# Splitting all 34 weight tiles once and loading every one of them in tile 1

## Chip, core and metric

One Trainium2 chip, one core. The metric is the device time of one execution in microseconds (us), the median of several executions. TensorE is called PE, VectorE DVE, ScalarE ACT, GpSimd POOL; SP is the queue that issues nearly all DMAs.

## What is computed

A block of a streaming encoder on 2048 positions and 1024 channels, in float32. Cut to what matters:

```python
h = rmsnorm(x, w_norm_pre)
proj = h @ w_in                       # 1024 x 3328: 26 weight tiles
q_a, k_a, v_a, z_a, q_r, f_r, i_r, z_r = jnp.split(proj, SPLIT_POINTS, axis=-1)
o_a = sliding_window_sink_attention(rope(q_a), rope(k_a), v_a, sinks) * silu(z_a)
o_r = rmsnorm(hgrn2_chunkwise(q_r, f_r, i_r, lb), hgrn_norm) * silu(z_r)
y = concat([o_a, o_r]) @ w_out        # 1024 x 1024: 8 weight tiles
x = x + rmsnorm(y, w_norm_post)
```

## The kernel before

The sequence is cut into 4 tiles of 512 positions (`t` from 0 to 3). Each tile passes over the weights, which are cut into weight tiles of 128 partitions x 1024 elements (0.5 MB): 26 of `w_in` (steps 0 to 25) and 8 of `w_out` (steps 26 to 33). In tiles 2 and 3 the output projection runs over 14 prepared tiles instead of 8 (`FAST`). A matmul of full float32 precision is made of three in the rounded type fp32r: every operand is split into a high half (rounded) and a low half (the rest), and the products high x high, low x high and high x low are summed in PSUM. One step is 24 matmuls of 512 columns (L596; L605 for `w_out`), with small matmuls of attention and recurrence put between them by `between`.

**Weight tiles are numbered through:** i = 34 t + w in tiles 0 and 1. A tile that is split passes through these hands:

- `load_raw(i)` (L445, issued by SP): the float32 tile goes from DRAM to one of 4 raw slots. It first waits until tile i - 4 has been split.
- `split_hi(i)` (L919, ACT, instruction L924): the high half is rounded into slot `SPLIT_SLOT[i]` of `w_hi`. It waits for three things: that PE has finished with the tile that had the slot before (`wait_slot`, L384), that this tile's halves have landed in DRAM if they are saved (`wait_saved`, L379), and that the raw tile has landed.
- `split_lo(i)` (L1257, DVE, instruction L1263): raw minus high goes to the same slot of `w_lo`.
- `save_split(i)` (L453, SP, issues L458): both halves are written to the DRAM tensors `kept_hi` and `kept_lo`, two DMAs of 0.5 MB. It waits for the split.

From number `FRESH` on, tiles aren't split. `load_split` (L461, SP, issues L469) loads both halves back from `kept`, two DMAs of 0.5 MB, after the same two waits, `wait_slot` and `wait_saved`. PE waits for one or the other in `wait_split` (L396).

There are 4 slots for halves. In tile 0 from tile 28 on only three of them are used: tiles 28, 29, 30 are in slots 0, 1, 2, so are 31, 32, 33, and the first three of tile 1 (34, 35, 36) take slots 0, 1, 2 again; 37 takes slot 3, which tile 27 had. The early waits of PE in tile 1 are thus for slots that became free three steps before.

Before, `LATE` is 6: saves begin with tile 6, and tile 1 splits its first six tiles (34 to 39) a second time and then saves them as rows 0 to 5 of `kept`. In tile 1's step 6 (i = 40 = `FRESH`) the loads begin.

**The order on SP** is that of the program and nothing passes anything else. For every i it holds `load_raw(i)`, then `save_split(i - 4)`, then, from `FRESH` on, `load_split`. Between them stand the tables of rope (at step 4 of tile 0, L499 and L500), the next tile's x (from step 10) and the residual rows (L512), whose first half is issued at step 31 of tile 0 and waits for DVE's L1253 in step 28.

ACT and DVE also run in program order. ACT does the splits of step s in `splits(t, s)` (L148): tile 34 at step 32 of tile 0, 35 at step 33, 36 and 37 after the squares of y at the end of tile 0 (L1225), 38 and 39 in steps 1 and 2 of tile 1. Five stores of the output of tile 0 (L1232, 2 MB in all) are issued on ACT's own DMA queue after those of 36 and 37.

The core of the program of SP:

```python
def load_raw(i):
    if i >= RAW_SLOTS:
        sp.wait_ge(lo_split.sem, lo_split.after(0, 0) + i - RAW_SLOTS)
...
def wait_saved(engine, i):
    slot = SPLIT_SLOT[i]
    engine.wait_ge(w_saved[slot], 32 * uses(slot, LATE, min(i, FRESH)))
```

Of the kernel before, what the change touches and what calls it, by code (L numbers as in the profile page):

```python
# [55 lines left out]
RAW_SLOTS = 4  # L56
# [22 lines left out]
def index(t, w):  # L79
    return t * WT + w if t < FAST else FAST * WT + (t - FAST) * FAST_WT + w  # L80
# [7 lines left out]
def tiles_of(t):  # L88
    return WT if t < FAST else FAST_WT
# [52 lines left out]
def split_at(s):  # L142


    return [w for w in (s + 2, s + 3) if w - s == (2 if w % WT in (0, 1, 2, 31, 32, 33) else 3)]


def splits(t, s):  # L148

    return [t * WT + w for w in split_at(s) if 3 < t * WT + w < FRESH]  # L150


LATE = 6
FRESH = WT + LATE

DVE_LOW = range(4, FRESH)
# [33 lines left out]
def hybrid_block(nc, x, x_rows, weights, cos, sin, vectors, w_post, squares, out, kept):  # L190
# [3 lines left out]
    with ctx:  # L194
# [180 lines left out]
        def uses(slot, start, end):  # L375

            return SPLIT_SLOT[start:end].count(slot)
# [6 lines that stand above are left out]
# [49 lines left out]
        def _(sp):  # L433
            def load_x(tile, k):


                if k == 0:
                    sp.wait_ge(h_lo_done.sem, h_lo_done.after(tile - 1, -1))
                    sp.wait_ge(x_squared.sem, x_squared.after(tile - 1, -1))
                    sp.wait_ge(finished.sem, finished.after(tile - 2, -1))  # L440
                    sp.wait_ge(finished_pool.sem, finished_pool.after(tile - 2, -1))
                sp.dma_start(x_in[:, k:k + 2, :],
                             x[bass.ts(tile, P), k * N:(k + 2) * N].rearrange("p (k n) -> p k n", n=N)).then_inc(x_quarter[k // 2], 16)
# [5 lines that stand above are left out]
                w, slot = i % WT, i % RAW_SLOTS  # L449
                sp.dma_start(w_raw[:, slot, :, :],  # L450
                             weights[w * P:(w + 1) * P, :].rearrange("p (k m) -> p k m", k=KT)).then_inc(w_loaded[slot], 16)

            def save_split(i):  # L453

                w, slot = i % WT, SPLIT_SLOT[i]
                sp.wait_ge(lo_split.sem, lo_split.after(0, 0) + i)
                for part, rows in ((w_hi, kept[0]), (w_lo, kept[1])):
                    sp.dma_start(rows[w * P:(w + 1) * P, :].rearrange("p (k m) -> p k m", k=KT),  # L458
                                 part[:, slot, :, :].bitcast(FP32)).then_inc(w_saved[slot], 16)

            def load_split(tile, w):  # L461

                slot, row = SPLIT_SLOT[index(tile, w)], rows_of(tile, w)
                wait_slot(sp, index(tile, w))
                wait_saved(sp, index(tile, w))
                if w == P7A and tile == FAST:
                    sp.wait_ge(t_saved, 16 * 2 * T_TILES)
                for part, rows in ((w_hi, kept[0]), (w_lo, kept[1])):
                    sp.dma_start(part[:, slot, :, :].bitcast(FP32),  # L469
                                 rows[row * P:(row + 1) * P, :].rearrange("p (k m) -> p k m", k=KT)).then_inc(w_ready[slot], 16)  # L470

            def load_sums(j):

                if j == 0:
                    sp.wait_ge(lo_split.sem, lo_split.after(0, 0) + FRESH - 1)
                else:
                    sp.wait_ge(t_saved, 16 * T_TILES)
                for r, w in enumerate((B11, B21, B12, B22)):
                    sp.dma_start(w_raw[:, r, :, :], weights[(w + j) * P:(w + j + 1) * P, :].rearrange("p (k m) -> p k m", k=KT)).then_inc(t_raw, 16)

            def save_sums(j, first):

                sp.wait_ge(t_high, 4 * j + first + 2)
                sp.wait_ge(t_low, 4 * j + first + 2)
                for r, w in ((0, T1), (2, T3)) if first == 0 else ((3, T2), (1, T4)):
                    rows = slice((w + j) * P, (w + j + 1) * P)
                    sp.dma_start(kept[0][rows, :].rearrange("p (k m) -> p k m", k=2), t_hi[j][r].bitcast(FP32)).then_inc(t_saved, 16)
                    sp.dma_start(kept[1][rows, :].rearrange("p (k m) -> p k m", k=KT), w_raw[:, r, :, :]).then_inc(t_saved, 16)
# [8 lines left out]
            def load_tables(t):  # L497
                sp.wait_ge(roped.sem, roped.after(t - 1, -1))
                sp.dma_start(cos_t[:, :], cos[bass.ts(t, P), :]).then_inc(tables_loaded, 16)  # L499
                sp.dma_start(sin_t[:, :], sin[bass.ts(t, P), :]).then_inc(tables_loaded, 16)  # L500
# [32 lines left out]
            for t in range(TILES):  # L533
                for w in range(tiles_of(t)):
                    i = index(t, w)
                    if FIRST_SPLIT <= i < FRESH:
                        load_raw(i)
                    if LATE + RAW_SLOTS <= i <= FRESH:
                        save_split(i - RAW_SLOTS)
                    if i == FRESH + 1:  # L540
                        for late in range(FRESH + 1 - RAW_SLOTS, FRESH):
                            save_split(late)
                    if i >= FRESH:
                        load_split(t, w)
                    if t == 0 and w == RAW_SLOTS:
                        load_tables(0)
                    if w - H0 in range(0, KT, 2) and t + 1 < TILES:
                        load_x(t + 1, w - H0)
                    if w == OUT0 and t + 1 < TILES:
                        load_tables(t + 1)  # L550
                    if (t, w) in SUMS_IN:
                        load_sums(SUMS_IN.index((t, w)))
                    for j in range(2):
                        for first in (0, 2):
                            if (t, w, first) in SUMS_OUT[j]:
                                save_sums(j, first)
                    if w == 1 and t > FAST:
                        load_residual(t - 1, 0)
                        load_residual(t - 1, 1)
                    if w == RAW_SLOTS - 1 and t > FAST:  # L560
                        store_y(t - 1, STORES)
                    if w == RES_AT[t][0]:
                        load_residual(t, 0)
                    if w == RES_AT[t][1]:
                        load_residual(t, 1)
# [6 lines left out]
        def _(pe):  # L572
# [219 lines left out]
            def unit_waits(t, n, w, k, i):  # L792

                if w not in [v for v, _, _ in UNITS[:n]]:
                    wait_split(pe, t, w)
# [442 lines left out]
        def _(dve):  # L1238
# [18 lines left out]
            def split_lo(i):  # L1257
                dve.wait_ge(hi_split.sem, hi_split.after(0, 0) + i)
                if i in (DVE_LOW.start, DVE_LOW.stop):

                    dve.wait_ge(lo_split.sem, lo_split.after(0, 0) + i - 1)
                s = SPLIT_SLOT[i]
                dve.tensor_tensor(w_lo[:, s, :, :], w_raw[:, i % RAW_SLOTS, :, :], w_hi[:, s, :, :], ALU.subtract).then_inc(lo_split.sem, 1)  # L1263
# [265 lines left out]
            for t in range(TILES):  # L1529
                links[0] = 0  # L1530
                for s in range(WT):
                    q, odd = divmod(s - SCORES0, 2)
                    h_of, kind = divmod(s - 1 - H0, 4) if H0 < s <= OUT0 else (0, None)
# [116 lines left out]
                            sum_head(t, h)  # L1650
                    if t == FAST and 0 <= s - SUMS_AT < 4:
                        sum_weights(1, s - SUMS_AT)
                    for i in splits(t, s) if (t, s) != (1, 0) and (t or kind not in (0, 1)) else ():
                        if i in DVE_LOW:
                            split_lo(i)

# [10 lines left out]
                for b in range(4):  # L1667
                    if b == 3 and t + 1 < TILES:
                        dve.wait_ge(x_high, t + 1)
                        dve.tensor_tensor(mix_lo[:, 0, :], x_acc[:, :], mix_hi[:, 0, :], ALU.subtract).then_inc(x_low, 1)  # L1670
                    if b == 3 and t == 0:
                        for i in splits(1, 0):
                            split_lo(i)
                    copy_y(t, 1, b)
                    if b == 0:
                        dve.wait_ge(res_loaded, t * 32 + 32)
                    dve.wait_ge(y_rstd.sem, y_rstd.after(t, b))
                    dve.wait_ge(y_read.sem, y_read.after(t, 4 + b))
                    for half in range(b in Y_POOL, 2):
                        finish_y(t, b, half)  # L1680
# [129 lines left out]
```

## Time and profile before

| | |
|---|---|
| median of 3 executions | 864.86 us (864.5 to 866.69) |
| profiled execution, its own time | 864.57 us |
| span of its instructions | 862.7 us |
| outside the span | 1.87 us |
| instructions | 12445 |
| moved by DMA | 211.20 MB |

The span runs from the first to the last instruction of the profiled execution; 1.87 us of its own time lie outside it. The profiled execution lies 0.29 us under the median. The timeline view gives starts in us from the span's start. Landing times are given by the DMA view as us from issue to landing.

### The profile page before, as it was taken

The page shows a single profiled execution, that of the slowest core. Times are in us where ns is not written, and L with a number is a line of the kernel's source. Part 1 is how long each engine was busy: PE and PEld are TensorE (multiplying, and loading weights), DVE is VectorE, ACT ScalarE, POOL GpSimd, SP SyncE. Part 2 cuts the span into 40 slices and gives each one's busy share as a digit, 9 for nine tenths or more (in the row PEclk, how much of TensorE's full clock was granted, in tenths as well). Part 3 has the DMA queues.
Part 4 walks back from the last instruction along what each step waited for, and adds up shares of the span by engine and source line. Part 5 has one row for each costly group of instructions (what it writes and reads, how often), then busy time and mean ns, then how long its engine had stood idle before and what let it go on. Part 6 is the DMA issues. An engine that isn't in the chain of part 4 may idle for free.

```text
span 862.7 us, 12445 instructions
## 1 busy us (share of the span) xinstructions
PE 851.9 (99%) x4428; PEld 700.6 (81%) x4428; DVE 631.9 (73%) x1125; ACT 519.0 (60%) x1033; POOL 114.6 (13%) x84
## 2 busy tenths in 40 slices
PE   8999999999999999999999999999999999999997
PEld 6787788888888778888888878888888887888885
DVE  6878878674656799767747789887775368888846
ACT  7766445763466458567446655865853755576544
POOL 0000013430200000332020000144300000004220
PEclk9999999999999999999999999999999999999999
DMA  8686755748986647464898785445699674444586
GB/s 322 212 325 221 244 205 170 285 147 314 418 342 248 213 145 265 152 210 133 321 382 348 276 330 172 146 151 216 241 374 396 228 273 147 147 147 158 189 326 254
DMA packets 59981, 211.20 MB, mean 245 GB/s; under 512 B 6672, under 2 KB 6928, under 8 KB 59920
## 3 DMA queue, kind: packets, MB, share of 16 engines
q1 hardware_dynamic: 57904, 205.56, 65.3%
q10 hardware_dynamic: 2016, 4.85, 1.4%
q8 instruction: 35, 0.57, 0.3%
q14 instruction: 26, 0.21, 0.1%
HBM read 157.95 MB, written 52.43 MB: 244 GB/s over the span
## 4 chain that ended last, share of the span: by engine, by line
PE 84%; DVE 9%; ACT 4%; issue 3%; DVEq 0%
PE bank L596 55%; PE bank L605 5%; PE turn_b L852 3%; PE score_b L852 3%; PE bank L852 3%; PE score_b L605 3%; PE turn_b L605 3%; PE turn_b L653 2%; DVE kv_tok L1386 2%; PE score_b L629 2%; PE turn_b L706 2%; PE bank L697 1%; PE bank L687 1%; PE turn_b L709 1%; ACT probs_t L951 1%
## 5 line engine op out<-in xcount | busy, mean ns | idle before, releaser
L596 PE MATMUL bank<-h_hi,w_lo 128*128 128x512 f32 x832 | 326.9, 393 | 0.0
L596 PE MATMUL bank<-h_lo,w_hi 128*128 128x512 f32 x832 | 326.3, 392 | 0.0
L596 PE MATMUL bank<-h_hi,w_hi 128*128 128x512 f32 x832 | 324.4, 391 | 0.5 <-issue 0.5
L596 PEld LDWEIGHTS bank<-h_lo,w_hi 128*128 128x128 f32 x832 | 156.4, 188 | 34.7 <-issue 3.3
L596 PEld LDWEIGHTS bank<-h_hi,w_hi 128*128 128x128 f32 x832 | 156.4, 188 | 33.1 <-issue 1.0
L596 PEld LDWEIGHTS bank<-h_hi,w_lo 128*128 128x128 f32 x832 | 156.3, 188 | 32.8
L1716 POOL TENSOR_TENSOR mix_lo<-v_r,mix_hi 128x512 fp32r<-128x512 f32 x16 | 21.2, 1322 | 539.0 <-ACT v_r L1142 539.0
L1263 DVE TENSOR_TENSOR w_lo<-w_raw,w_hi 128x1024 fp32r<-128x1024 f32 x36 | 44.8, 1248 | 34.6 <-ACT w_hi L924 34.1
L1386 DVE STREAM_TRANSPOSE kv_tok<-k_mid 32x128 f32<-32x128 f32 x192 | 58.1, 303 | 2.8
L924 ACT ACTIVATE w_hi<-w_raw 128x1024 fp32r<-128x1024 f32 x38 | 39.8, 1051 | 24.9 <-issue 10.2
L1700 POOL TENSOR_TENSOR x_acc<-x_acc,x_sq 128x512 f32<-128x512 f32 x21 | 32.7, 1557 | 70.0 <-ACT x_sq L974 70.0
L928 ACT ACTIVATE g_a<-g_b 128x512 f32<-128x512 f32 x30 | 18.9, 630 | 38.2 <-DVE g_b L1340 38.2
L939 ACT ACTIVATE g_a<-g_a 128x512 f32<-128x512 f32 x32 | 20.2, 632 | 34.6 <-DVE g_a L1344 34.6
L1068 ACT ACTIVATE f_b<-bank 32x512 f32<-32x512 f32 x48 | 28.3, 589 | 15.6 <-PE bank L596 9.7
L960 ACT ACTIVATE kv_tok<-f_d 32x128 f32<-32x128 f32 x96 | 29.5, 307 | 10.0 <-DVE f_d L1580 8.9
L1344 DVE SCALAR_TENSOR_TENSOR g_a<-g_b,g_a 128x512 f32<-128x512 f32 x30 | 21.7, 723 | 18.3 <-ACT g_a L930 18.3
L960 ACT ACTIVATE probs<-f_d 32x128 f32<-32x128 f32 x96 | 29.5, 307 | 1.2
L1637 DVE TENSOR_TENSOR_SCAN f_c<-reset,f_b 128x512 f32<-128x512 f32 x16 | 19.6, 1225 | 11.3 <-ACT f_b L1125 11.3
L1479 DVE SCALAR_TENSOR_TENSOR q_gate<-q_gate,y_stats,x_in 128x512 f32<-128x512 f32 x28 | 23.1, 873 | 4.4 <-DMA x_in<-in_x_rows 3.5
L605 PE MATMUL bank<-w_hi,mix_lo 128*128 128x512 f32 x64 | 25.3, 395 | 0.0
L605 PE MATMUL bank<-w_hi,mix_hi 128*128 128x512 f32 x64 | 24.9, 390 | 0.0
L605 PE MATMUL bank<-w_lo,mix_hi 128*128 128x512 f32 x64 | 24.9, 389 | 0.0
(280 smaller groups left out, 1549.2 us busy)
## 6 DMA issues: line engine op xcount, KB each, us to landing
w_hi<-kept_hi SPq DMA_DIRECT2D x108, 512.0 KB, 3.8
w_lo<-kept_lo SPq DMA_DIRECT2D x108, 512.0 KB, 4.9
w_raw<-in_weights SPq DMA_DIRECT2D x46, 512.0 KB, 6.2
kept_hi<-w_hi SPq DMA_DIRECT2D x34, 512.0 KB, 6.3
kept_lo<-w_lo SPq DMA_DIRECT2D x34, 512.0 KB, 7.4
x_in<-in_x_rows SPq DMA_DIRECT2D x8, 1024.0 KB, 8.1
x_in<-in_x SPq DMA_DIRECT2D x15, 512.0 KB, 6.6
kept_lo<-w_raw SPq DMA_DIRECT2D x8, 512.0 KB, 7.0
```

The source lines that it names most:

```text
L596: mm = pe.matmul(acc(w)[:, :], stationary[:, s, k, :], moving[:, k, :], start=(m == 0), stop=(m == 3 * KT - 1), skip_group_check=True)
L605: mm = pe.matmul(y_bank[half][b][:, :], mix[:, k, b * P:(b + 1) * P], weight[:, SPLIT_SLOT[index(t, w)], (k % 2) * 4:(k % 2) * 4 + 4, :].r ...
L852: mm = pe.matmul(into, mix, weight, start=w in (P1A, P7A, P2A, P4A) and k == 0 and part == 0, stop=k == KT // 2 - 1 and part == 2, skip_gr ...
L924: act.activation(w_hi[:, SPLIT_SLOT[i], :, :], w_raw[:, i % RAW_SLOTS, :, :], ACT.Copy).then_inc(hi_split.sem, 1)
L960: copy = act.activation(square(v_tok(t, h), j, i), square(f_d[:, :], i, j), ACT.Copy)
L1068: copy = act.activation(dst[32 * b:32 * b + 32, :], acc(s - 1)[32 * (b ^ 1):32 * (b ^ 1) + 32, :], ACT.Copy)
L1263: dve.tensor_tensor(w_lo[:, s, :, :], w_raw[:, i % RAW_SLOTS, :, :], w_hi[:, s, :, :], ALU.subtract).then_inc(lo_split.sem, 1)
L1344: dve.scalar_tensor_tensor(g_a[:, :], g_b[:, :], 0.0, gate_log(t, i), ALU.min, ALU.subtract).then_inc(gate_arg.sem, 1)
L1386: last = dve.transpose(square(kv_tok[:, 0, :], j, i), square(k_mid[:, :], i, j))
L1479: dve.scalar_tensor_tensor(y, y, y_scale[:, b:b + 1], x_in[:, 2 * b + half, :], ALU.mult, ALU.add).then_inc(finished.sem, 1)
L1700: pool.tensor_tensor(x_acc[:, :], x_acc[:, :], x_sq[:, :], ALU.add).then_inc(x_added.sem, 1)
L1716: pool.tensor_tensor(o_sq_lo, o_sq[:, :], o_sq_hi, ALU.subtract).then_inc(o_low.sem, 1)
```

## The change

`LATE` becomes 0 and so `FRESH` 34: the saves begin with tile 0, and every tile from 34 on is loaded. All 34 saves are of tile 0's splits; those of tiles 0 to 5 are issued in its steps 4 to 9. The last four saves are placed anew: 30 and 31 at i = 34 ahead of the load of 34, 32 at i = 35 ahead of the load of 35, 33 at i = 36 ahead of the load of 36. The split code for tile 1 goes.

```diff
-LATE = 6
+LATE = 0
 FRESH = WT + LATE
...
                     if LATE + RAW_SLOTS <= i <= FRESH:
                         save_split(i - RAW_SLOTS)
-                    if i == FRESH + 1:
-                        for late in range(FRESH + 1 - RAW_SLOTS, FRESH):
-                            save_split(late)
+                    if FRESH <= i < FRESH + 3:
+                        save_split(i - 3)
                     if i >= FRESH:
                         load_split(t, w)
...
-                    for i in splits(t, s) if (t, s) != (1, 0) and (t or kind not in (0, 1)) else ():
+                    for i in splits(t, s) if t or kind not in (0, 1) else ():
                         if i in DVE_LOW:
                             split_lo(i)
...
-                    if b == 3 and t == 0:
-                        for i in splits(1, 0):
-                            split_lo(i)
```

## Rows read from the trace of the kernel before

**Rows 1.** The page, busy time by engine and the chain that ended last.

```profile
PE 851.9 (99%) x4428; PEld 700.6 (81%) x4428; DVE 631.9 (73%) x1125; ACT 519.0 (60%) x1033; POOL 114.6 (13%) x84
...
PE 84%; DVE 9%; ACT 4%; issue 3%; DVEq 0%
```

**Rows 2.** PE's waits: us in total, times, longest us.

```profile
PE bank L861 <- DVE ones_r L1265: 3.5, 1, 3.5
```

**Rows 3.** Timeline of PE, first matmuls of steps 0, 1, 2 of tile 1 (start us, us).

```profile
226.28 0.39 PE L596 MATMUL bank<-h_hi,w_hi 128*128 128x512 f32 x1
...
231.72 0.39 PE L596 MATMUL bank<-h_hi,w_hi 128*128 128x512 f32 x1
...
237.62 0.39 PE L596 MATMUL bank<-h_hi,w_hi 128*128 128x512 f32 x1
```

**Rows 4.** The page, costliest groups: the two instructions of a split.

```profile
L1263 DVE TENSOR_TENSOR w_lo<-w_raw,w_hi 128x1024 fp32r<-128x1024 f32 x36 | 44.8, 1248 | 34.6 <-ACT w_hi L924 34.1
...
L924 ACT ACTIVATE w_hi<-w_raw 128x1024 fp32r<-128x1024 f32 x38 | 39.8, 1051 | 24.9 <-issue 10.2
```

**Rows 5.** Timeline of SP, end of tile 0: low half of the save of 31.

```profile
210.31 0.43 SPq L458 DMA_DIRECT2D kept_lo<-w_lo  x1
```

**Rows 6.** DMAs issued from 209.4 to 210.5 us: count, KB, us to landing.

```profile
kept_lo<-w_lo SPq DMA_DIRECT2D x1, 512.0 KB, 11.0
```

**Rows 7.** Timeline of ACT: the split of tile 34, [idle before <- releaser].

```profile
221.37 1.06 ACT L924 ACTIVATE w_hi<-w_raw 128x1024 fp32r<-128x1024 f32 x1 [2.69 <-DMA kept_lo<-w_lo]
```

**Rows 8.** Windows view, 198 to 240 us: busy of each engine, clock, DMA share, GB/s.

```profile
198.00:240.00 42.00, 42.00 (x187) 34.79 (x186) 22.41 (x28) 16.63 (x36) 5.74 (x4) 1.00 1.01 402
```

**Rows 9.** DMAs issued from 264.9 to 265.5 us: one pair of loads alone.

```profile
w_hi<-kept_hi SPq DMA_DIRECT2D x1, 512.0 KB, 3.7
w_lo<-kept_lo SPq DMA_DIRECT2D x1, 512.0 KB, 5.2
```

**Rows 10.** DMAs issued from 61.4 to 62.4 us: a raw load with a save behind it.

```profile
w_raw<-in_weights SPq DMA_DIRECT2D x1, 512.0 KB, 4.2
...
kept_lo<-w_lo SPq DMA_DIRECT2D x1, 512.0 KB, 5.9
```

**Rows 11.** A save issued between 228.6 and 232.5 us; the page's median; the first store of y.

```profile
kept_lo<-w_lo SPq DMA_DIRECT2D x1, 512.0 KB, 8.6
...
kept_lo<-w_lo SPq DMA_DIRECT2D x34, 512.0 KB, 7.4
...
231.12 0.35 ACTq L1232 DMA_DIRECT2D out<-q_gate  x1
```

**Rows 12.** Windows view, 12 to 40 us, columns as in rows 8.

```profile
12.00:40.00 28.00, 27.93 (x122) 22.48 (x121) 23.61 (x36) 24.46 (x39) 0.00 (x0) 1.00 0.72 255
```

**Rows 13.** DMAs issued from 12.1 to 13.1 us: raw tile 4 and a table.

```profile
w_raw<-in_weights SPq DMA_DIRECT2D x1, 512.0 KB, 4.9
```

**Rows 14.** Timelines of SP, ACT, DVE and PE, start of tile 0.

```profile
12.58 0.43 SPq L499 DMA_DIRECT2D cos_t<-in_cos  x1
...
21.11 1.05 ACT L924 ACTIVATE w_hi<-w_raw 128x1024 fp32r<-128x1024 f32 x1
...
33.82 1.06 ACT L924 ACTIVATE w_hi<-w_raw 128x1024 fp32r<-128x1024 f32 x1
...
26.47 0.69 DVE L1322 TENSOR_TENSOR cos_t<-cos_t,x_scale 128x512 f32<-128x512 f32 x1 [0.48 <-ACT x_scale L966]
...
27.80 0.69 DVE L1326 TENSOR_TENSOR f_a<-bank,cos_t 128x512 f32<-128x512 f32 x1
...
31.19 0.39 PE L596 MATMUL bank<-h_hi,w_hi 128*128 128x512 f32 x1
```

**Rows 15.** Timeline of PE at its start and its end; the last window's clock.

```profile
7.71 0.77 PE L596 MATMUL bank<-h_hi,w_hi 128*128 128x512 f32 x1
...
856.22 0.39 PE L852 MATMUL turn_b<-w_lo,s_hi 128*128 128x512 f32 x1
...
857.00:862.70 5.70, 0.00 (x0) 0.92 0.75 289
```

## The prediction

> **What bounds the kernel now.** I read the page first: PE is busy for 99% of the span, no other engine for more than 73%, and the chain that ended last is PE's for 84% [rows 1]. The view of PE's waits then shows where it stands still: the largest entry by far is one of 3.5 us, before its first instruction [rows 2]. The timeline confirms it at the place that the change touches: step 0 of tile 1 starts at 226.28 us and step 1 at 231.72, which is 24 matmuls at 0.227 us each, the pitch at which they follow each other where nothing is in their way [rows 3]. So PE computes almost without a pause. The change takes no matmul away. Anything removed from ACT, DVE or the DMA queues is worth nothing by itself; anything that makes PE wait is added in full.
>
> **What is removed.** Six splits: 6 x 1.05 = 6.3 us on ACT and 6 x 1.25 = 7.5 us on DVE [rows 4]. PE covers both, so I count 0; their cover would be gone only where PE waits, and there neither is late. Six raw loads (3 MB) go too. What gets earlier is tile 0's y: ACT no longer splits tile 34 at 221.37 us [rows 7] and 35 after it, before the second half's squares, nor 36 and 37 before the stores of the output. PE doesn't wait for those today, so this is 0 as well, but the 2 MB of stores will come some 3 us earlier than today and meet the new loads.
>
> **What is moved to the start.** Six saves (6 MB) now stand in SP's steps 4 to 9. From 198 to 240 us the DMA engines are full at 402 GB/s [rows 8]; half a megabyte takes 1.3 us at that rate, and where three such transfers follow each other the third lands 2.55 us after the first, 1.27 each [rows 10]. I take 1.25. Raw tile 4, issued 0.37 us ahead of the first table at 12.58 [rows 14], lands 4.9 us later at 17.1 [rows 13]. The save of tile 0 follows it: 17.1 + 2.5 = 19.6 us. Three may now wait for it. The tables, behind it: 19.6 + 1.25 = 20.9, and DVE reads them at 26.47. ACT's split of tile 4, which needs tile 0's slot saved, runs at 21.11. Then raw 5, save 1, raw 6, save 2, raw 7, save 3 are 9 transfers, 11.25 us: save 3 lands at 32.1, or 33.6 with the 0.6 MB that ACT's own queue loads then (masks and norm weights, L1035 and L1037), and ACT's split of tile 7 runs at 33.82 [rows 14]. Everything is in time, if closely. In the 28 us from 12 to 40 the engines are 72% busy [rows 12], so 7.8 us of the 15 us that are added find room there and the rest runs on into a stretch where each split still has four steps. I cost it at 0. The bounds: no gain; as a loss the rival on tile 0's start below.
>
> **What is new: a chain of saves and loads at the start of tile 1.** Today tiles 34 to 39 come through raw slots, whose loads need no halves slot. After the change tile 34's load must wait until tile 31's save, from the same slot, has landed. And SP issues in order: save 32 stands behind load 34, load 35 waits for save 32, save 33 stands behind load 35, and load 36 waits for save 33. Three transfers that used to lie side by side come one after the other, each with its full latency.
>
> The first link: save 31's low half is issued at 210.31 us today [rows 5] and lands 11.0 us later, at 221.3 [rows 6]; ACT's split of 34, released by a save of the low half, starts at 221.37 and confirms it [rows 7]. It queues behind raw tiles 34 and 35, which go: 221.3 - 2 x 1.25 = 218.8 us. What comes before it isn't changed: the residual rows, which hold up SP at step 31, and the saves up to 30.
>
> A pair of loads alone: the high half lands 3.7 us after its issue, the low half, issued about 0.4 later, after 5.2; 5.6 us for the pair [rows 9]. A load pair with a save pair behind it isn't in the trace with idle engines before it. The nearest is a raw load with a save, 1.5 MB: the low half, issued 0.85 us after the raw load, lands 5.9 us on [rows 10], 6.75 in all. That is 3 x 1.25 us of transfer and 3.0 us fixed. For 2 MB: 5.0 + 3.1 = 8.1 us, the 3.1 taken from the load pair (5.6 - 2.5), which is how every such link begins. Bounds for the link: 7 us (a fixed part of 2) and 9 us (some store among it).
>
> - Load 34: issued 218.8, lands 224.4. PE wants it at 226.28 [rows 3]: in time by 1.9 us.
> - Save 32 lands at 218.8 + 8.1 = 226.9. Load 35 lands at 226.9 + 5.6 = 232.5. PE wants it at 231.72: **0.8 us of waiting**.
> - Save 33: 226.9 + 8.1 = 235.0 without the output stores. Those are issued from 231.12 us on today; the save issued just ahead of them took 8.6 us against a median of 7.4, one store more [rows 11]. I take one store: 236.3. Load 36: 236.3 + 5.6 = 241.9. All that is then issued since 226.9 (load 35, save 33, stores, load 36) is 12.5 us of transfer, and 226.9 + 12.5 + 3.1 = 242.5 is when it would land if every store went first. Between both: 242.3. PE wants it at 237.62: **4.7 us in total**, of which 0.8 are already had.
>
> Tile 37 is loaded right behind 36, two transfers later, 244.8, and is wanted at 242.3 + 5.4 + a bit: in time. Tiles 38 and on have their slots free and no save to wait for. Bounds of the sum: without any store in the way 240.6, 3.0 us; with all 5 us of stores ahead of save 33, 245.7, 8.1 us. I keep 4.7, nearest to the rows that show how a save and a store mix.
>
> **Sum:** 864.57 (the profiled execution) + 0 + 4.7 = 869.3 us. It lies 0.29 us under the median, so 869.5 is what I put against 864.86, +0.5%.
>
> **Rival 1: the links are short and PE doesn't wait.** This ends on the other side. From 218.8 to 237.62 there are 18.8 us for two links and a pair of loads, which I make 21.8 and, with stores, 23.5. If the fixed part is about 1 us shorter per link than in rows 9 and 10, and stores keep out of the way, what is left is under 1 us: 865 us. For it: with nothing else in flight the engines answer faster. Against it: the pair of rows 9 had them to itself and shows 3.1 us of fixed part. 13%, a tenth of it or so below 864.9 by more than the noise. The Trainium skill, DMA: Bandwidth & Descriptors, "Latency and other measured facts", puts the fixed cost at about 2 us and says that it shrinks with the load on the memory; by its figure (an estimate) each link loses 1 us and the stall would be about 1.7 us, 866.5 us.
>
> **Rival 2: the clock falls during the stall.** PE has not stood still once before. At 7.71 us a matmul still takes 0.77 us, twice the 0.39 of later ones, so 1.2 GHz held from its first instruction at 3.5 to about 8.3 us (7.71 and one slow matmul), 4.8 us [rows 2, 15]. If the stall of about 4 us brought 1.2 GHz back, about 4.8 us would run at half speed: 2.4 us more, 872 us. Against it: after the last matmul at 856.22 the window from 857 on still shows a mean clock of 0.92 [rows 15], that is 0.9 us at half level at its end, so 5 us of standing still passed at 2.4 GHz. 10%. The Trainium skill, TensorE: Matmul & The Clock Gate, Part 1, says that an idle array goes back to half its clock; by that rule the clock could fall in a stall of this length.
>
> **Rival 3: the early saves hold up tile 0.** ACT's split of tile 4 waits for save 0. PE's step 4 needs the bank that DVE's L1326 reads at 27.80 + 0.7 and starts at 31.19: 2.7 us of room, 3.1 with DVE's idle 0.48 [rows 14]. If save 0 lands later than 24.2 us, that room is spent; a landing at 26.9 costs 2.7 us, 872 us with the rest. 8%.
>
> **The change doesn't do what it says:** the saves' number and rows stay 34 whatever the code says; I see in the diff that they do. 2%, same time.
>
> **The numbers.** The forecast (waiting of 3.0 to 8.1 us, 868 to 873) has 67%. A measurement of this kernel can tell 0.3%, 2.6 us, from nothing: up to 862.3 is faster, from 867.5 slower. Slower takes the forecast, rivals 2 and 3 and a little of rival 1: 0.85; same 0.13; faster 0.02. The range has to leave out no more than 2 in 10: from 866.0, inside rival 1, to 873.0, the far end of the stores' bound.
>
> **What would show it.** In the changed kernel's profile: PE's waits gain two entries at L596, released by DMA `w_lo<-kept_lo`, of about 0.8 and 4 us, for tiles 35 and 36, and step 2 of tile 1 starts at about 242. SP's waits show L458's landings (kept_lo) before the loads, about 8 us apart. The clock stays at 1.00. Up to 226 us every PE step starts as today, within 0.5 us. DMA moves 214 MB (211.2 + 6 - 3), and 6 splits are gone on either engine: L924 x32, L1263 x30. It is wrong if PE waits for nothing there (links short), if tile 0's steps 4 to 8 start later than today (rival 3), or if the waiting lies in a step that I call in time.

## The result and the profile after

The changed kernel takes 874.36 us (median of 6, 872.93 to 876.56) against 865.30 before (6 executions beside them); the ratio is 1.0105, 95% interval 1.009 to 1.012. It is slower by 9.1 us where 4.6 us were forecast, and lies outside the range of 866 to 873.

The profiled execution took 874.30 us with a span of 872.5 us, 9.8 more than before. The page shows the work that was forecast and a slightly smaller busy share of PE:

```profile
PE 856.0 (98%) x4428; PEld 702.7 (81%) x4428; DVE 625.9 (72%) x1119; ACT 513.6 (59%) x1027; POOL 114.6 (13%) x84
...
DMA packets 60845, 214.34 MB, mean 246 GB/s; under 512 B 6768, under 2 KB 7024, under 8 KB 60784
...
PE 71%; DVE 12%; ACT 6%; DMA 5%; issue 4%; SPq 2%; POOL 0%; DVEq 0%; ACTq 0%
...
L1262 DVE TENSOR_TENSOR w_lo<-w_raw,w_hi 128x1024 fp32r<-128x1024 f32 x30 | 37.7, 1256 | 26.9 <-ACT w_hi L923 26.4
L923 ACT ACTIVATE w_hi<-w_raw 128x1024 fp32r<-128x1024 f32 x32 | 33.6, 1051 | 15.5 <-issue 11.2
```

DMA now has a share of 5% in the chain that ended last, where it had none [rows 1], and six splits are gone on either engine [rows 4]. The view of PE's waits names what took the time (us in total, times, longest us; its entry of 3.5 us before the first instruction is as before), and that of SP's waits what stands behind it:

```profile
PE bank L595 <- DMA w_lo<-kept_lo: 5.0, 1, 5.0
PE turn_b L583 <- DMA w_lo<-kept_lo: 0.5, 1, 0.5
```

```profile
SPq L382 <- DMA kept_lo<-w_lo: 25.4, 3, 9.4
```

PE has two new waits, both for a load's low half, and SP has three for a save's landing, 25.4 us in total. They are the chain of the prediction. PE's timeline has them at the steps that the prediction named:

```profile
232.27 0.39 PE L595 MATMUL bank<-h_lo,w_hi 128*128 128x512 f32 x1
237.71 0.80 PE L595 MATMUL bank<-h_hi,w_hi 128*128 128x512 f32 x1 [5.05 <-DMA w_lo<-kept_lo]
238.30 0.63 PE L595 MATMUL bank<-h_hi,w_lo 128*128 128x512 f32 x1
...
243.42 0.57 PE L595 MATMUL bank<-h_hi,w_lo 128*128 128x512 f32 x1
...
246.79 0.50 PE L583 MATMUL turn_b<-mix_hi,ones_r 128*128 128x512 f32 x1 [0.51 <-DMA w_lo<-kept_lo]
...
247.36 0.40 PE L595 MATMUL bank<-h_hi,w_hi 128*128 128x512 f32 x1
```

Step 1 of tile 1 starts at 237.71 us instead of 231.72, step 2 at 247.36 instead of 237.62 [rows 3]. From there to the end the distance to the kernel before stays within 0.1 us of 9.8. So the ledger is: 0.8 us at the start of tile 0, 5.2 at tile 35 (step 1), 3.8 more up to step 2. The matmuls between show durations of about 0.6 us until 243.4 instead of 0.39, which is the second surprise. The windows view of that stretch (busy of PE, PEld, DVE, ACT, POOL, then granted clock, DMA share, GB/s):

```profile
232.50:237.70 5.20, 0.16 (x1) 0.00 (x0) 1.31 (x2) 2.35 (x4) 0.00 (x0) 0.93 1.02 412
237.70:242.00 4.30, 4.29 (x10) 3.43 (x11) 0.00 (x0) 0.00 (x0) 0.00 (x0) 0.50 0.70 281
242.00:244.00 2.00, 2.00 (x6) 1.54 (x6) 0.00 (x0) 0.00 (x0) 0.00 (x0) 0.55 0.51 168
244.00:247.30 3.30, 2.79 (x12) 1.99 (x12) 0.00 (x0) 0.00 (x0) 0.00 (x0) 1.00 0.97 366
```

The granted clock fell from 2.4 to 1.2 GHz in PE's wait: 0.93 as the mean of the first 5.2 us puts the fall at 237.0 us, 4.3 us after PE's last matmul had ended at 232.7. Step 1 took 8.2 us from its first matmul to its last instead of 5.2. And while PE waits, the DMA engines are full (412 GB/s). The timelines of SP and ACT's queue say with what:

```profile
220.17 0.32 SPq L469 DMA_DIRECT2D w_hi<-kept_hi  x1
...
221.48 0.43 SPq L458 DMA_DIRECT2D kept_lo<-w_lo  x1
229.06 0.32 SPq L469 DMA_DIRECT2D w_hi<-kept_hi  x1
...
232.00 0.76 SPq L458 DMA_DIRECT2D kept_lo<-w_lo  x1
241.81 0.32 SPq L469 DMA_DIRECT2D w_hi<-kept_hi  x1
```

```profile
228.37 0.35 ACTq L1231 DMA_DIRECT2D out<-q_gate  x1
```

The loads of 34, 35 and 36 are issued at 220.17, 229.06 and 241.81, each when the save before it has landed. The first store of tile 0's output is issued at 228.37, 2.8 us earlier than before [rows 11] and ahead of load 35. The DMA view for what was issued from 229.0 to 229.5, for save 33, and for load 36 (count, KB, us to landing):

```profile
w_lo<-kept_lo SPq DMA_DIRECT2D x1, 512.0 KB, 8.2
out<-q_gate ACTq DMA_DIRECT2D x1, 512.0 KB, 7.0
...
kept_lo<-w_lo SPq DMA_DIRECT2D x1, 512.0 KB, 9.8
...
w_hi<-kept_hi SPq DMA_DIRECT2D x1, 512.0 KB, 3.7
w_lo<-kept_lo SPq DMA_DIRECT2D x1, 512.0 KB, 4.6
```

Load 35's low half, issued at 229.42, lands after 8.2 us at 237.6, save 33's at 232.00 + 9.8 = 241.8, load 36's at 242.18 + 4.6 = 246.8.

### The profile page after: what moved, and what is told of

Same layout as the page of the kernel before. It is cut to its first block, busy times and chain, and to the rows that moved or that the text cites. A ratio compares the mean times of both kernels' runs of the same rounds, so it can differ in the third digit from the quotient of the medians.

```text
span 872.5 us, 12439 instructions
## 1 busy us (share of the span) xinstructions
PE 856.0 (98%) x4428; PEld 702.7 (81%) x4428; DVE 625.9 (72%) x1119; ACT 513.6 (59%) x1027; POOL 114.6 (13%) x84
## 4 chain that ended last, share of the span: by engine, by line
PE 71%; DVE 12%; ACT 6%; DMA 5%; issue 4%; SPq 2%; POOL 0%; DVEq 0%; ACTq 0%
PE bank L595 49%; DMA kept_lo<-w_lo 3%; PE turn_b L851 3%; PE score_b L851 3%; PE bank L604 2%; PE bank L851 2%; DVE kv_tok L1385 2%; PE turn_b L652 2%; PE score_b L628 2%; PE turn_b L705 1%; PE turn_b L604 1%; PE score_b L604 1%; PE turn_b L708 1%; PE bank L696 1%; PE bank L686 1%
## 5 line engine op out<-in xcount | busy, mean ns | idle before, releaser
L1262 DVE TENSOR_TENSOR w_lo<-w_raw,w_hi 128x1024 fp32r<-128x1024 f32 x30 | 37.7, 1256 | 26.9 <-ACT w_hi L923 26.4
L923 ACT ACTIVATE w_hi<-w_raw 128x1024 fp32r<-128x1024 f32 x32 | 33.6, 1051 | 15.5 <-issue 11.2
L1252 DVE SCALAR_TENSOR_TENSOR h_lo<-x_in,vec,h_hi 128x512 fp32r<-128x512 f32 x32 | 23.3, 774 | 3.4 <-ACT h_hi L977 3.4
L1339 DVE TENSOR_TENSOR g_b<-bank,x_scale 128x512 f32<-128x512 f32 x32 | 21.8, 682 | 4.7 <-PE bank L595 4.1
```

The source lines that it names most:

```text
L923: act.activation(w_hi[:, SPLIT_SLOT[i], :, :], w_raw[:, i % RAW_SLOTS, :, :], ACT.Copy).then_inc(hi_split.sem, 1)
L1252: dve.scalar_tensor_tensor(h_lo[:, k, :], x_in[:, k, :], w_pre[:, k:k + 1], h_hi[:, k, :], ALU.mult, ALU.subtract).then_inc(h_lo_done.sem, 1)
L1339: dve.tensor_tensor(g_b[:, :], acc(w)[:, :], x_scale[:, :], ALU.mult).then_inc(tile_read.sem, 1)
```

## The experiments

All but `early_saves_alone` start from the changed kernel. "Before" is run beside each group on the same chip and had medians of 864.93 to 865.20 us.

### Is it the order? Both saves ahead of the loads

```diff
-                    if FRESH <= i < FRESH + 3:
-                        save_split(i - 3)
+                    for late in {FRESH: (31, 32), FRESH + 1: (33,)}.get(i, ()):
+                        save_split(late)
```

> The changed kernel with saves 31 and 32 ahead of load 34 and save 33 ahead of load 35, so that no load stands between two saves. Theory (the chain of save, load, save, load, save, load on SP makes the loss): save 31 still lands at about 220, but save 32 lands at about 223 and save 33 at about 228; loads 35 and 36 are issued then and land before PE wants them or within 1 us of it. Time 865 to 867 us, PE's waits for w_lo<-kept_lo at most 1 us. Rival (the bytes at the boundary are what is too much, in whatever order): load 36 still lands near 246 and the time stays at 872 to 875 us.

864.90 us (864.62 to 866.45), ratio to before 1.000 (0.9991 to 1.0009). The whole loss is gone, with the same bytes. The timeline of SP in this kernel:

```profile
214.01 0.69 SPq L458 DMA_DIRECT2D kept_lo<-w_lo  x1
219.71 0.32 SPq L469 DMA_DIRECT2D w_hi<-kept_hi  x1
...
221.02 0.43 SPq L458 DMA_DIRECT2D kept_lo<-w_lo  x1
222.19 0.32 SPq L469 DMA_DIRECT2D w_hi<-kept_hi  x1
...
228.23 0.32 SPq L469 DMA_DIRECT2D w_hi<-kept_hi  x1
```

Save 32 is issued at 214.0 instead of 221.5, so load 35 goes at 222.2 and load 36 at 228.2, 13.6 us earlier than in the changed kernel. Step 2 of tile 1 starts at 238.45, 0.8 us after the kernel before [rows 3], as every step since step 4 of tile 0. Load 36's low half took 8.3 us among the same stores, and nothing waited for it. The theory holds, the rival falls.

### How large is each link? One save ahead

```diff
+                    for late in {FRESH: (31, 32), FRESH + 2: (33,)}.get(i, ()):
+                        save_split(late)
```

> The changed kernel with only save 32 moved ahead of load 34; save 33 stays between loads 35 and 36. Theory: one link of the chain is gone. Save 32 lands near 222, load 35 near 229 (wanted at 232.5), save 33 near 231 to 233, load 36 near 237 to 239 (wanted at 238.4): loss 0 to 1 us, 865 to 866.5 us. Rival (both saves must be ahead): load 36 lands at 241 or later, 868 us or more.

868.25 us (866.06 to 869.82), ratio 1.0031 (1.0018 to 1.0045). That is above the 865 to 866.5 us that I expected, and as slow as the rival's 868, though load 36 landed before the rival's 241. One link taken out brings back most of the loss, but not all. Save 33 landed at 232.0 as forecast, but load 36 behind it met the stores and took 8.5 us, landing at 240.45; PE waited 1.9 us for it:

```profile
PE turn_b L583 <- DMA w_lo<-kept_lo: 1.9, 1, 1.9
```

Step 2 of tile 1 starts 3.4 us after the kernel before, 1.2 of it from the start of tile 0. Another 0.6 us is lost late in tile 2, 0.4 of it in a wait for a weight load. Why, isn't known.

The other one alone puts save 33 behind save 32 and ahead of load 35:

```diff
+                    for late in {FRESH: (31,), FRESH + 1: (32, 33)}.get(i, ()):
+                        save_split(late)
```

> The changed kernel with save 33 moved ahead of load 35, behind save 32, which stays behind load 34. Theory: load 35 still waits for save 32, landed near 229, and lands at 235 to 237, wanted at 232.5; load 36 follows when save 33 has landed, near 231.5, so right behind load 35, and lands at 238 to 241, wanted some 5.5 us after load 35's landing. PE waits 3 to 5 us, most of it for tile 35: 868.5 to 870.5 us. Rival (only the last link counts): 865 to 866.5 us.

872.89 us (872.05 to 874.26), 3.4 us above the middle of what I expected. The landings are near the theory's (load 35 at 237.25, load 36 at 241.5), the time is not. PE waited 5.6 us for tile 35 and then nothing for 36; the windows view from the end of its standstill on (PE busy, clock, DMA share, GB/s):

```profile
237.50:241.00 3.50, 3.50 (x9) 0.50 1.04 418
241.00:246.00 5.00, 5.00 (x20) 0.80 0.79 323
```

The clock was at half until 243.0 us. Tile 36's halves were there 4.5 us before step 2 began at 245.98, so nothing hid the slow matmuls here.

### What do the output stores add?

```diff
+                    if t == 0:
+                        act.wait_ge(w_ready[SPLIT_SLOT[WT + 2]], 32)
                     for b, cols, pieces, pool_pieces in PLAIN_STORES if t < FAST else ():
```

> The changed kernel in which ACT holds tile 0's five output stores back until tile 36's halves have landed, so that none of their 2 MB meets loads 35 and 36 or save 33. Theory (chain plus stores): a load lands 5.7 us after its issue and a save 8 to 8.8 us after the load ahead of it, so load 35 lands near 234.8, save 33 near 237.5, load 36 near 242.6 and step 2 of tile 1 starts about 5 us late instead of 9.7: 869.5 to 871 us. Rival (links are long without the stores too): load 36 lands at 245 or later, 873 us or more.

869.44 us (868.69 to 871.43), 4.9 us less than the changed kernel and at the lower end of what I expected. The DMA view of the new load 35, save 33 and load 36, issued at 228.12 to 228.48, 228.96 to 230.76 and 236.32 to 236.68:

```profile
w_lo<-kept_lo SPq DMA_DIRECT2D x1, 512.0 KB, 5.3
...
kept_lo<-w_lo SPq DMA_DIRECT2D x1, 512.0 KB, 5.5
...
w_lo<-kept_lo SPq DMA_DIRECT2D x1, 512.0 KB, 4.5
```

Load 35 landed at 233.8 (5.7 us for the pair), save 33 at 236.3 (8.2 us after the save before it) and load 36 at 241.2: the theory's links, and the 240.6 us that the prediction had worked out without stores. PE waited only 1.8 us for tile 35, and the clock still fell.

Making the stores small instead of late was less clean (most of tile 0's output is left out):

```diff
+                        if t == 0:
+                            act.dma_start(out[bass.ds(b * P, P), cols[0] * N:cols[0] * N + 128],
+                                          q_gate[:, 2 * b + cols[0], 0:128]).then_inc(stored[b // 2], 16)
+                            continue
```

> The changed kernel in which the five stores of tile 0's output on ACT's queue write 64 KB each in place of 256 or 512 KB (most of tile 0's output is left out), so 1.7 MB less at the boundary. Theory (the stores lengthen two links of the chain): load 35 lands some 5.7 us after its issue instead of 8.6, save 33 lands near 237.5 instead of 241.8 and load 36 near 243 instead of 246.8; the time falls by 3.5 to 4.5 us, to 870 to 871 us. Rival (the fixed part of each link makes the loss, not the stores): less than 1 us gained, 873.5 to 875 us.

871.98 us (869.02 to 873.21), 2.4 less than the changed kernel where 3.5 to 4.5 were expected. Load 36 landed at 243.3 as the theory has it, 3.5 us earlier, but load 35 still took 7.1 us as a pair, so the small stores of 512 bytes per partition weren't free; and the profiled execution lost another 1.0 us late in tile 2, 0.7 of it in a wait for a weight load, which I leave unexplained. The direction is the theory's, the size short of it.

### Do the early saves cost anything?

The kernel before, with its first six saves early; tiles 34 to 39 are split again and not saved:

```diff
-                    if LATE + RAW_SLOTS <= i <= FRESH:
+                    if RAW_SLOTS <= i < WT + RAW_SLOTS:
                         save_split(i - RAW_SLOTS)
-                    if i == FRESH + 1:
-                        for late in range(FRESH + 1 - RAW_SLOTS, FRESH):
-                            save_split(late)
...
-            engine.wait_ge(w_saved[slot], 32 * uses(slot, LATE, min(i, FRESH)))
+            engine.wait_ge(w_saved[slot], 32 * uses(slot, 0, min(i, WT)))
```

> The kernel before, with its first six saves moved to steps 4 to 9 of tile 0 (its 34 saves are those of tiles 0 to 33); tile 1 still splits its first six tiles a second time and doesn't save them. Theory: the early saves cost nothing or up to 0.8 us at the start of tile 0 and nothing later, since each split waits for a save that has landed: 865 to 866.3 us. Rival (they hold up tile 0 or load its queues for long): tile 1 starts 2 us or more late, 867.5 us or more.

865.77 us (864.71 to 866.35), ratio 1.0003 (0.9995 to 1.0012): no difference that can be measured. Its profiled execution starts tile 1 1.3 us later than that of before, but that distance is there from step 1 of tile 0 on, ahead of anything that the early saves can delay, and shrinks by 0.3 up to step 4. Most of it is a clock that rose later at the start of the program, as PE's timeline shows, first of this kernel and then of the kernel before:

```profile
10.92 0.63 PE L593 MATMUL bank<-h_hi,w_lo 128*128 128x512 f32 x1
...
11.37 0.40 PE L596 MATMUL bank<-h_hi,w_lo 128*128 128x512 f32 x1
```

From 8.6 to 11.6 us PE did 8 matmuls here and 15 in the kernel before. The start of tile 0 varies by as much between the profiled executions of all these kernels (step 1 from 0.5 earlier to 1.5 later than before). Of the changed kernel's 0.8 us, 0.4 is there at step 1. The rest appears between 22 and 26 us, and in that stretch the other kernels with early saves, this one included, move by -0.3 to +0.3 us. So neither part is shown to be a cost of the early saves.

### Does the fallen clock cost anything?

```diff
+                    if (t, w) == (1, 1):
+                        pe.wait_ge(y_read.sem, y_read.after(1, 3 - 8))
+                        for _ in range(20):
+                            pe.matmul(acc(1)[:, :], ones_r[:, :], h_hi[:, 0, :], start=True, stop=True)
                     wait_split(pe, t, w)
```

> The changed kernel with 20 matmuls of 512 columns whose result is overwritten (4.5 us at full clock) ahead of PE's wait for tile 35's halves, so that PE doesn't stand still there for 5 us and its clock stays at 1.00. Theory (the landing of tile 36's halves at about 246.8 sets the loss, and the 3 us that PE lost at half clock lay beside that wait): the time stays within 0.5 us, 873.8 to 874.9 us, and PE waits longer for tile 36 than before, by some 3 us. Rival (the clock's fall adds to the loss): 3 us less, 871 to 871.5 us.

874.61 us (872.76 to 875.01): unchanged, as the theory has it, but the profile shows that it is no clean proof. The clock stayed full through step 1 and fell in step 2 instead, after PE's 2.7 us of waiting for tile 36, as PE's timeline shows:

```profile
245.11 0.50 PE L583 MATMUL turn_b<-mix_hi,ones_r 128*128 128x512 f32 x1 [2.73 <-DMA w_lo<-kept_lo]
...
245.91 0.42 PE L595 MATMUL bank<-h_hi,w_lo 128*128 128x512 f32 x1
246.14 0.61 PE L595 MATMUL bank<-h_lo,w_hi 128*128 128x512 f32 x1
```

Step 2 took 1.65 us longer for it, and load 36 had landed 1.7 us earlier than in the changed kernel. The two cancel. (1.1 of the 1.7 us were already there when save 31 landed, long before the fill began.) So both waits were filled, the second with 12 matmuls more:

```diff
-                    if (t, w) == (1, 1):
-                        pe.wait_ge(y_read.sem, y_read.after(1, 3 - 8))
-                        for _ in range(20):
-                            pe.matmul(acc(1)[:, :], ones_r[:, :], h_hi[:, 0, :], start=True, stop=True)
+                    if (t, w) in ((1, 1), (1, 2)):
+                        pe.wait_ge(y_read.sem, y_read.after(1, (3, 1)[w - 1] - 8))
+                        for _ in range((20, 12)[w - 1]):
+                            pe.matmul(acc(w)[:, :], ones_r[:, :], h_hi[:, 0, :], start=True, stop=True)
```

> As fill_wait, and 12 more matmuls of 512 columns (2.7 us) ahead of PE's wait for tile 36, so that its clock stays full in both waits. Theory: step 2 starts when tile 36's halves have landed, 245 to 247 us, and no matmul runs at half clock afterwards, which in fill_wait cost 1.65 us: 872.5 to 874 us, between that and the changed kernel itself because the landing sets it. Rival (the clock's fall is 3 us of the loss): 871 us or less.

872.92 us (872.09 to 874.81), clock 1.00 throughout the boundary in the profile. Within the theory's 872.5 to 874, outside the rival's 871 or less. The fill itself, at its end at 244.7, outlasts the landing at 244.2 by half a microsecond. By the medians the changed kernel takes 1.4 us less with a full clock, or 1.9 without that excess, but the intervals of the two ratios overlap (1.0081 to 1.0115 and 1.009 to 1.012), and in this profile load 36 landed 2.6 us earlier (244.2 against 246.8), 1.6 of it already at save 31's landing. So no part of the difference is shown to be the clock's; its share is at most some 2 us, not 3.

The clean case is `only_33_ahead`, where nothing waits behind the slow step. The same 20 matmuls there, added to that kernel by the same lines as in `fill_wait`:

```diff
+                    if (t, w) == (1, 1):
+                        pe.wait_ge(y_read.sem, y_read.after(1, 3 - 8))
+                        for _ in range(20):
+                            pe.matmul(acc(1)[:, :], ones_r[:, :], h_hi[:, 0, :], start=True, stop=True)
```

> only_33_ahead with 20 matmuls of 512 columns (4.5 us) ahead of PE's wait for tile 35, whose result is overwritten, so that the clock stays full. There tile 36's halves land long before PE is done with tile 35 at half clock, so no second wait hides the fall. Theory (a fall costs about 2.9 us where nothing waits behind it): tile 35 lands at about 237 as before, its step then takes 5.4 instead of 8.3 us, and the time falls by 2.4 to 3.0 us, from 872.9 to about 870 us. Rival (the landings alone set the time, as in fill_wait): within 0.7 us of 872.9.

869.92 us (869.30 to 871.36) against 872.89: 3.0 us. In the profiles the stretch from the start of step 1 to that of step 2 takes 5.9 us (236.75 to 242.65) instead of 8.7 (237.28 to 245.98), which is 2.8 us for the clock alone. The same windows of this kernel as of `only_33_ahead` above:

```profile
237.50:241.00 3.50, 3.50 (x17) 1.00 1.03 415
241.00:246.00 5.00, 5.00 (x23) 1.00 1.04 422
```

17 matmuls in 3.5 us instead of 9. The Trainium skill, TensorE: Matmul & The Clock Gate, Part 1, says that an idle array goes back to half its clock; the traces agree: 0.50 after PE stood still for 5.6 us, 1.00 where the wait was filled.

### A second cure: the fourth slot

```diff
-SPLIT_SLOT = [s for r in (4, 4, 4, 4, 4, 4, 4, 3, 3) for s in range(r)]
+SPLIT_SLOT = [i % 4 for i in range(34)]
...
-SPLIT_SLOT += [w % 4 for w in range(WT)] + [(WT + w) % 4 for w in range(FAST_WT)] * (TILES - FAST)
+SPLIT_SLOT += [(WT + w) % 4 for w in range(WT)] + [(2 * WT + w) % 4 for w in range(FAST_WT)] * (TILES - FAST)
```

> The changed kernel, its order on SP untouched, with the tiles of halves going round all four slots without a break (34 takes the slot of 30 instead of 31, 35 that of 31, 36 that of 32). Theory (a load that waits for the save issued just before it makes the chain): now each load waits for a save issued one place earlier, which has landed or is about to. Load 34 is issued near 217, load 35 near 220, load 36 near 226 and lands near 232, before it is wanted: no loss at the boundary, 865 to 866.3 us, and PE's waits show no w_lo<-kept_lo over 0.5 us. Rival (the order, save 32 and 33 behind loads, is bad by itself): 868 us or more.

866.37 us (864.55 to 866.88), ratio 1.0003 (0.9994 to 1.0012). SP's order is that of the changed kernel and the loss is gone all the same, since no load waits for the save issued just ahead of it. Load 36 goes at 224.8:

```profile
216.28 0.32 SPq L469 DMA_DIRECT2D w_hi<-kept_hi  x1
...
218.77 0.32 SPq L469 DMA_DIRECT2D w_hi<-kept_hi  x1
...
224.80 0.32 SPq L469 DMA_DIRECT2D w_hi<-kept_hi  x1
```

PE's waits name no `kept_lo` in it. Neither this nor `saves_ahead` is faster than the kernel before: PE's work is the same and it sets the time.

## Why the prediction was wrong

**Right:** PE sets the time, and what ACT and DVE lose (6 splits each) is worth nothing. The early saves cost nothing that can be measured. One sign of being wrong did appear, since tile 0's steps start 0.8 us late instead of within 0.5, but `early_saves_alone` shows no loss, and rival 3 falls. The loss is the chain save 31, load 34, save 32, load 35, save 33, load 36; tile 34 is in time, tiles 35 and 36 are late, nothing after them is, and moving two saves ahead of two loads removes all of it. Rival 1 falls too: the links aren't shorter than the 8.1 us taken from the rows, but 8.9 (save 31 to save 32) and 12.8 us (save 32 to save 33).

**Wrong, the term for the stores.** The step that failed is "I take one store". By the prediction's own steps:

| | predicted | measured | without stores (`late_y_stores`) |
|---|---|---|---|
| save 31 lands | 218.8 | 220.05 | 219.1 |
| save 32 lands | 226.9 | 229.0 | 228.1 |
| load 35 lands | 232.5 | 237.6 | 233.8 |
| save 33 lands | 236.3 | 241.8 | 236.3 |
| load 36 lands | 242.3 | 246.8 | 241.2 |

The link from save 32's landing to save 33's was put at 9.4 us and measured 12.8; with the stores held back it was 8.2. The difference of 4.6 us is nearly the 5 us that 2 MB take. I had seen that the stores come some 3 us earlier, and then priced them by the save of [rows 11]. But that save was issued ahead of every store, the first of which came at 231.12, and two more came before it landed at 237.2. The kernel before:

```profile
228.67 0.83 SPq L458 DMA_DIRECT2D kept_lo<-w_lo  x1
...
232.32 0.35 ACTq L1232 DMA_DIRECT2D out<-q_gate  x1
234.02 0.34 ACTq L1232 DMA_DIRECT2D out<-q_gate  x1
```

So the row wasn't one store met by one save, and it doesn't have the case of the changed kernel, where the stores begin ahead of load 35 (228.37 against 229.06) and of save 33 (231.18). There they land from 232.9 to 242.1 us, four of the five before save 33 at 241.8, and load 36, which isn't issued until then, can't share the time with them. My check by total bytes (242.5) had load 36 already queued while the stores ran, which the chain itself forbids. The bound that I set aside, all 5 us of stores ahead of save 33, was nearly the case: 8.1 us against 9.2 measured at load 36's landing (246.8 - 237.62), of which 0.8 is tile 0's later start.

The stores are the largest part of the miss, but not all. Load 36 landed 4.5 us after 242.3: save 31 landed 1.3 late (0.8 of it tile 0's start), the first link took 0.8 more than 8.1 without any store in it (8.9 to 9.0 us in `late_y_stores` too), the second 3.4 more than 9.4, and load 36 1.0 less than the 6.0 left for it.

**Wrong, the clock.** Rival 2 had 10% and happened. The evidence against it was the end of the program, where 5 us of standing still passed at 2.4 GHz [rows 15]; 4.3 us were enough at the boundary, and 1.8 us in `late_y_stores`. That end was one sample, and an unusual one. In the changed kernel the last matmul ends at 866.40, and the clock has fallen two microseconds later:

```profile
866.50:868.40 1.90, 0.00 (x0) 0.00 (x0) 1.90 (x4) 1.13 (x4) 0.00 (x0) 1.00 0.98 381
868.50:872.50 4.00, 0.00 (x0) 0.00 (x0) 1.52 (x3) 0.00 (x0) 0.00 (x0) 0.50 0.67 262
```

Over the ends of all twelve profiles it fell 2.0 to 5.2 us after the last matmul, and the kernel before has the longest. At the boundary the fall cost at most some 2 us, less than its price of 2.4, because PE would have waited for tile 36 in any case: at full clock step 1 would have ended near 243.1 us, 3.7 before the landing. `fill_both` gives the 2 us as a bound; where nothing hides the fall, it costs 2.8 to 3.0.

## What to carry over

Where a load reuses a buffer whose old content must first be saved, let it wait only for a save that was issued at least one load earlier, by moving the save up (`saves_ahead`) or with one more buffer (`four_slots`). A load that waits for the save just ahead of it pays the full latency of both in every round, here 8 to 13 us against a step of 5.4. When an engine is relieved, ask what its transfers will now collide with, and charge all their bytes to a chain that waits for the last of them. A chain of waits doesn't share time with other traffic the way a queue of transfers does, so a check by total bytes is a lower bound of it. And a row prices a collision only if the transfers stood in the same order in it: look at which was issued first.

## What was not expected of the hardware

PE's clock can fall after a short wait. In `late_y_stores` PE stood still for 1.8 us, resumed, and 0.9 us later ran at half clock for 3.4 us. Its timeline and then its windows:

```profile
233.81 0.50 PE L595 MATMUL bank<-h_hi,w_hi 128*128 128x512 f32 x1 [1.80 <-DMA w_lo<-kept_lo]
```

```profile
234.70:238.10 3.40, 3.40 (x10) 2.61 (x9) 0.00 (x0) 0.00 (x0) 0.00 (x0) 0.50 0.27 80
```

In `only_32_ahead` PE waited 1.9 us and the clock stayed at 1.00 in the profile. So a wait of some 2 us may or may not bring the fall, and stretches at half clock lasted 3.4 us in `fill_wait`, `small_y_stores` and `late_y_stores` and 6.8 us in the changed kernel and `only_33_ahead`, where PE stood still for 5 us and more. What decides between them is open.
